# Keeping the delta-rule inverse as 32x32 blocks and transposing it on the vector engine

## The reference

```
L = where(strict, (k_beta @ k.T) * decay, 0)
T = triangular_solve(eye + L, eye, lower=True, unit_diagonal=True)   # the inverse of I + L
u = T @ v_beta ;  w = T @ (k_beta * exp(g_cum))
# then, chunk by chunk: v_new = u - w @ state; o = qd @ state + qk @ v_new; state = ...
```

## Time and profile before

| | before |
|---|---|
| median of 3 runs | 2057.83 us (2057.76 to 2059.85) |
| span of the profiled execution | 2055.0 us |
| the median less that span | 2.8 us |
| heads 0 to 7 of the recurrence | about 549 to 885 us of the span, one each 43.5 us |

### The profile page before, as it was taken

The page is one execution under the profiler, slowest core; times in us unless marked ns, Lnnn a source line. Parts: engine busy times, 40 slices in busy tenths (PEclk is TensorE's granted clock), DMA queues, the critical chain, the costliest instruction groups (busy, mean ns, idle before and its releaser), DMA issues.

```text
span 2055.0 us, 31779 instructions
## 1 busy us (share of the span) xinstructions
PE 2017.8 (98%) x12910; PEld 1621.5 (79%) x12910; DVE 1465.0 (71%) x2281; ACT 569.1 (28%) x994; POOL 354.7 (17%) x320
## 2 busy tenths in 40 slices
PE   8999999999999999999999999999999999999999
PEld 6888788887777777777778877777888888888887
DVE  5766666667877777667888887566656778949973
ACT  2000122222544444324774234444310010000000
POOL 2212111111101110011111211111112122212221
PEclk9999999999999999999999999999999999999999
DMA  4323222222211121122112332111223332322332
GB/s 161 112 92 103 83 90 86 93 83 75 83 60 57 63 68 61 60 72 82 62 63 73 126 98 88 62 48 45 77 82 103 98 103 92 103 92 93 102 97 88
DMA packets 53361, 173.73 MB, mean 85 GB/s; under 512 B 6336, under 2 KB 6720, under 8 KB 53088
## 3 DMA queue, kind: packets, MB, share of 16 engines
q1 hardware_dynamic: 48112, 161.67, 23.9%
q10 hardware_dynamic: 5104, 10.03, 1.8%
HBM read 169.51 MB, written 2.16 MB: 84 GB/s over the span
## 4 chain that ended last, share of the span: by engine, by line
PE 45%; DVE 6%; ACT 2%; issue 1%; DVEq 0%; ACTq 0%
PE ps_lin L1817 13%; PE ps_lin L1818 13%; PE ps_lin L1819 13%; PE ps_att L1863 4%; PE ps_aux L1863 2%; ACT arena L1271 2%; DVE arena L409 1%; DVE w_lo L409 1%; DVE arena L415 1%; DVE arena L897 1%; PE ps_att L1872 0%; DVE y_lo L409 0%; DVE sq L409 0%; DVE xw_lo L415 0%; DVE x L409 0%
## 5 line engine op out<-in xcount | busy, mean ns | idle before, releaser
L1817 PE MATMUL ps_lin<-xw_hi,w_hi 128*128 128x512 f32 (+1 forms) x1728 | 698.5, 404 | 0.0
L1819 PE MATMUL ps_lin<-xw_hi,w_lo 128*128 128x512 f32 (+1 forms) x1728 | 675.0, 391 | 0.0
L1818 PE MATMUL ps_lin<-xw_lo,w_hi 128*128 128x512 f32 (+1 forms) x1728 | 674.0, 390 | 0.0
L391 POOL TENSOR_SCALAR w_hi<-raw 128x1024 fp32r<-128x1024 f32 (+5 forms) x312 | 349.9, 1122 | 1685.1 <-PE ps_lin L1819 1560.5
L409 DVE TENSOR_TENSOR w_lo<-raw,w_hi 128x1024 fp32r<-128x1024 f32 (+2 forms) x344 | 382.3, 1114 | 48.0 <-POOL w_hi L391 17.6
L1271 ACT ACTIVATE arena<-arena 128x512 f32<-128x512 f32 (+7 forms) x331 | 206.4, 631 | 734.3 <-DVE arena L409 357.6
L1819 PEld LDWEIGHTS ps_lin<-xw_hi,w_lo 128*128 128x128 f32 (+1 forms) x1728 | 322.7, 187 | 71.8
L1817 PEld LDWEIGHTS ps_lin<-xw_hi,w_hi 128*128 128x128 f32 (+1 forms) x1728 | 323.1, 187 | 68.4 <-issue 3.7
L1818 PEld LDWEIGHTS ps_lin<-xw_lo,w_hi 128*128 128x128 f32 (+1 forms) x1728 | 323.4, 187 | 61.1
L409 DVE TENSOR_TENSOR arena<-ps_lin,rstd 128x512 f32<-128x512 f32 (+2 forms) x213 | 146.6, 688 | 201.2 <-PE ps_lin L1819 186.7
L1817 PE MATMUL ps_lin<-y_hi,w_hi 128*128 128x512 f32 (+1 forms) x544 | 205.4, 378 | 1.3 <-DVE w_lo L409 1.1
(11 more groups left out here) (175 smaller groups left out, 1697.2 us busy)
## 6 DMA issues: line engine op xcount, KB each, us to landing
raw<-in_w_up SPq DMA_DIRECT2D x44, 512.0 KB, 3.3
raw<-in_conv_w_in SPq DMA_DIRECT2D x32, 512.0 KB, 3.3
raw<-in_fox_w_in SPq DMA_DIRECT2D x32, 512.0 KB, 3.3
raw<-in_gdn_w_in SPq DMA_DIRECT2D x32, 512.0 KB, 3.2
raw<-in_w_gate SPq DMA_DIRECT2D x24, 512.0 KB, 3.2
raw<-in_swa_w_in SPq DMA_DIRECT2D x20, 512.0 KB, 3.2
raw<-in_w_ml SPq DMA_DIRECT2D x16, 512.0 KB, 3.3
raw<-in_w_down SPq DMA_DIRECT2D x16, 512.0 KB, 3.6
```

What stands on the lines that cost most here:

```text
L391: pool.tensor_scalar(w_whole(n, kc * c)[0], w_raw(n, kc * c), 1.0, 0.0, mult, add).then_inc(s("w_rounded"), 1)
L1817: pe.matmul(o, wh, hi, start=first and k == 0, stop=False)
L1818: pe.matmul(o, wh, lo, start=False, stop=False)
L1819: ins = pe.matmul(o, wl, hi, start=False, stop=last and k == kc - 1)
```

## The change

The inverse is kept as 32x32 blocks, in 32 columns a chunk, up to level 4. The products with the identity, their ScalarE copy and the products Y of levels 1 to 4 are gone. VectorE instead copies V into `Uc` itself and turns all 32x32 blocks of `Uc` with one transpose into `Ts`; it does so five times a head, for U0 and for levels 1 to 4. Z and V of levels 1 to 4 have 16 moving columns where they had 32. Level 5 uses 32x32 tiles, and level 6 takes its operands from the new 64x64 blocks `Th` and from `U`, which ScalarE (six diagonal copies and two more) and VectorE (one) put together at level 5. U0 is made by four operations on 32 partitions each where there were two on 64. At level 5 X takes two operations where it took one. The fill between the transpose of U0 and level 1 is gone; level 3 has one more. `LAST_PIECE` is moved to match. At head 0 four memsets stand where there was one.

```diff
-        LEVEL_FILL = (0, 2, 2, 1, 1, 2, 1)
+        LEVEL_FILL = (0, 2, 2, 2, 1, 2, 1)
-        LAST_PIECE.update({LAST_FILL + at: (3 + i // BANKS, i % BANKS) for i, at in enumerate((1, 2, 4, 5, 7, 8))})
+        LAST_PIECE.update({LAST_FILL + at: (3 + i // BANKS, i % BANKS) for i, at in enumerate((1, 3, 4, 6, 7, 9))})
...
 # VectorE, gdn_head
-                for top in (0, HD):
-                    step(tt(U0[top:top + HD], chunks(F["LT"])[top:top + HD, :, top:top + HD], over_chunks(mat("pairs0_ident")[top:top + HD, 0:HD], HD), mult))
-                tt(U0, U0, over_chunks(mat("pairs0_ident")[:, HD:]), add).then_inc(s("gdn_U0"), 1)
+                for at in range(0, P, SQ):
+                    last = tt(U0[at:at + SQ], chunks(F["LT"])[at:at + SQ, :, at:at + SQ], over_chunks(mat("pairs")[at:at + SQ, 0:SQ], SQ), mult)
+                step(last)
+                step(tt(U0, U0, over_chunks(mat("pairs")[:, SQ:2 * SQ]), add))
+                dve.transpose(F["Ts"], F["Uc"]).then_inc(s("gdn_T0"), 1)
...
-                fill(1)
...
+                    elif l == 5:
+                        ts(F["X"][l][SQ:HD, :], ps_att[SQ:HD, 2, 0:NT * SQ], -1.0, mult)
+                        ts(F["X"][l][HD + SQ:, :], ps_att[HD + SQ:, 2, 0:NT * SQ], -1.0, mult).then_inc(s("gdn_X"), 1)
...
-                        dve.wait_ge(s("gdn_TX"), 5 * h + l)
-                        tt(part(F["Tm"]), part(F["Tm"]), ps_att[:, 1, 0:P].rearrange("p (b d) -> p b d", d=d), add).then_inc(s("gdn_T"), 1)
+                        if l < 5:
+                            dve.wait_ge(s("gdn_XU"), 6 * h + l)
+                            step(dve.tensor_copy(part(F["Uc"], 1), new(ps_att[:, 3, :])))
+                            dve.transpose(F["Ts"], F["Uc"]).then_inc(s("gdn_T"), 1)
+                        else:
+                            dve.wait_ge(s("gdn_TX"), h + 1)
+                            dve.tensor_copy(chunks(F["Th"])[SQ:, :, 0:SQ], chunks(ps_att[SQ:HD, 1, 0:NT * SQ])).then_inc(s("gdn_T"), 1)
...
 # ScalarE, gdn_head
-                act.wait_ge(s("gdn_U0T"), h + 1)
-                activation(F["Tm"][:, 0:NT * HD], ps_att[:, 2, 0:NT * HD], ACT.Copy).then_inc(s("gdn_T0"), 1)
...
                     if l == 5:
+                        act.wait_ge(s("gdn_T"), 5 * h + 4)
+                        activation(Th[0:SQ, :, 0:SQ], Ts[0:SQ], ACT.Copy)
+                        activation(Th[SQ:, :, SQ:], Ts[SQ:HD], ACT.Copy).then_inc(s("gdn_Th"), 1)
+                        for at in range(0, P, SQ):
+                            activation(U[at:at + SQ, :, at:at + SQ], Uc[at:at + SQ], ACT.Copy)
...
 # TensorE, gdn_head
-                pe.wait_ge(s("gdn_U0"), h + 1)
-                for c in range(NT):
-                    for top in (0, HD):
-                        rows = slice(top, top + HD)
-                        last = mm(Z[rows, c * HD:(c + 1) * HD], F["Uc"][rows, c * HD:(c + 1) * HD], mat("ident")[rows, rows])
-                last.then_inc(s("gdn_U0T"), 1)
-                fill(1)
...
+                    squares = [(slice(b, b + SQ), slice(c * SQ, (c + 1) * SQ), slice(c * P + b, c * P + b + SQ), c) for c in range(NT) for b in range(0, P, SQ)]
+                    below = [(slice(b, b + SQ), slice(b + SQ, b + 2 * SQ), slice(c * SQ, (c + 1) * SQ), slice(c * P + b + SQ, c * P + b + 2 * SQ)) for c in range(NT) for b in (0, HD)]
...
+                    if l < 5:
+                        for rows, at, of, c in squares:
+                            last = mm(to(V[rows], c), F["X"][l][rows, at], half(F["Uc"][rows, at], 1))
+                    elif l == 5:
+                        for a_, b_, at, of in below:
+                            if b_.start == SQ:
+                                last = mm(Y[b_, at], F["Uc"][b_, at], F["X"][l][b_, at])
+                        last.then_inc(s("gdn_TX"), 1)
+                        for a_, b_, at, of in below:
+                            last = mm(V[a_, at], F["X"][l][b_, at], F["Uc"][b_, at])
```

More of the change, by code:

```diff
@@ L26 @@
 HD = 64
+SQ = 32
 FF = 2816
@@ L2018, in gdn_head @@
                 pe.wait_ge(s("gdn_vb"), h + 1)
-                pe.wait_ge(s("gdn_U0"), h + 1)
-                for c in range(NT):
-                    for top in (0, HD):
-                        rows = slice(top, top + HD)
-                        last = mm(Z[rows, c * HD:(c + 1) * HD], F["Uc"][rows, c * HD:(c + 1) * HD], mat("ident")[rows, rows])
-                last.then_inc(s("gdn_U0T"), 1)
-                fill(1)
                 for l in range(1, 7):
                     d = 1 << l
[L2028 to L2031, removed]
+                    squares = [(slice(b, b + SQ), slice(c * SQ, (c + 1) * SQ), slice(c * P + b, c * P + b + SQ), c) for c in range(NT) for b in range(0, P, SQ)]
+                    below = [(slice(b, b + SQ), slice(b + SQ, b + 2 * SQ), slice(c * SQ, (c + 1) * SQ), slice(c * P + b + SQ, c * P + b + 2 * SQ)) for c in range(NT) for b in (0, HD)]
+                    half = lambda ap, i: ap.rearrange("p (b two d) -> p b two d", two=2, d=d)[:, :, i, :]
+                    to = lambda ap, c: ap[:, c * SQ // 2:(c + 1) * SQ // 2].rearrange("p (b d) -> p b d", d=d)
                     if l == 1:
@@ L2035, in gdn_head @@
                         pe.wait_ge(s("gdn_T"), 5 * h + l - 1)
-                    if l < 6:
-                        for c, rows, b, off in tiles:
-                            last = mm(to(Z[rows], c), F["LT"][rows, c * P + b:c * P + b + n], half(F["Tm"][rows], c * HD, 0))
+                    if l < 5:
+                        for rows, at, of, c in squares:
+                            last = mm(to(Z[rows], c), F["LT"][rows, of], half(F["Ts"][rows, at], 0))
+                    elif l == 5:
+                        for a_, b_, at, of in below:
+                            last = mm(Z[b_, at], F["LT"][a_, of], F["Ts"][a_, at])
+                    else:
+                        pe.wait_ge(s("gdn_Th"), h + 1)
+                        for c in range(NT):
+                            last = mm(Z[HD:, c * HD:(c + 1) * HD], F["LT"][0:HD, c * P + HD:(c + 1) * P], F["Th"][:, c * HD:(c + 1) * HD])
@@ new lines, in gdn_head @@
+                    last.then_inc(s("gdn_XT"), 1)
+                    fill(1)
+                    if l == 5:
+                        pe.wait_ge(s("gdn_QK"), h + 1)
+                    elif l == 6:
+                        pe.wait_ge(s("gdn_U"), 2 * h + 1)
+                    pe.wait_ge(s("gdn_X"), 6 * h + l)
+                    if l < 5:
+                        for rows, at, of, c in squares:
+                            last = mm(to(V[rows], c), F["X"][l][rows, at], half(F["Uc"][rows, at], 1))
+                    elif l == 5:
+                        for a_, b_, at, of in below:
+                            if b_.start == SQ:
+                                last = mm(Y[b_, at], F["Uc"][b_, at], F["X"][l][b_, at])
+                        last.then_inc(s("gdn_TX"), 1)
+                        for a_, b_, at, of in below:
+                            last = mm(V[a_, at], F["X"][l][b_, at], F["Uc"][b_, at])
@@ L2049, in gdn_head @@
[L2049 to L2054, removed]
-                    else:
-                        for c in range(NT):
-                            last = mm(V[0:HD, c * HD:(c + 1) * HD], F["X"][l][HD:, c * HD:(c + 1) * HD], F["Uc"][HD:, c * HD:(c + 1) * HD])
+                            last = mm(V[0:HD, c * HD:(c + 1) * HD], F["X"][l][HD:, c * HD:(c + 1) * HD], F["U"][HD:, c * P + HD:(c + 1) * P])
```

59 lines of the change are left out of this document (25 added, 34 removed).

## The result

| | before | after |
|---|---|---|
| median of 17 runs each | 2056.68 us (2053.94 to 2059.85) | 2060.07 us (2053.17 to 2066.15) |
| ratio, 95% interval | | 1.0018 (1.0011 to 1.0025) |
| span of the profiled execution | 2055.0 us | 2058.3 us |

A forecast was written before the change was run, and what follows sets the result against it. TensorE was taken to set the pace; per middle head 2.80 us saved against 2.96 of waits. Six heads +1.0, head 0 +0.1, last head -1.2: -0.1 on the 2055.0 span, plus 2.8 around it, 2057.7 us; range 2044 to 2068.

The forecast's parts named there:

- The part on VectorE's order: Middle head: 2.80 us of TensorE savings against 2.96 us of new waits for VectorE at levels 1, 4 and 5.
- four operations on 32 partitions: VectorE making U0 ahead of the first X: four operations at 0.32 us each without overlap, 1.28 us.
- first LT to V of level 1: VectorE's stretch in a middle head from the first LT to the start of V of level 1: 5.63 us.
- wait ahead of V of level 1 / 4 / 5: TensorE idle for VectorE at three places of a middle head: 1.56, 0.54 and 0.86 us.
- level 5's saving in Y and V: TensorE at level 5 on 32x32 tiles: Y and V cost 0.91 us, which saves 0.36.
- a head, clock at 1.00: Length of a middle head with TensorE at 2.4 GHz: 43.63 us, a change of +0.17.
- Head 0: First head: no norm product at level 4 (-0.73 us), three more memsets ahead of X (about 0.65): +0.1 us.
- The last head: Last head: VectorE has no pieces, product-to-product latency rules; -1.2 us including 0.36 at level 5.
- my own case: Whole kernel: the forecast of 2057.7 us, with 2053 to 2062 as its own range, chance 0.42.
- The step that failed: Rival "much slower": new waits of 3 us in 43 let the clock fall to 1.2 GHz, over 2068 us, chance 0.06.
- All of it comes through: Rival: the waits fill with work taken to be in the way, about 2036 us, chance 0.12.
- Slower, by the transposes: Rival: a transpose of 4-byte words costs 0.69 us at three tight places a head, about 2066 us, chance 0.22.

The follow-up runs named there:

- experiment 1: Changed kernel with one extra 128x512 float32 product on TensorE in the wait for the first X, heads 0 to 6: 2051.38 us, ratio 0.9975.
- experiment 3: Changed kernel with VectorE's QK moved from in front of the first X to behind level 2's transpose: 2046.57 us, ratio 0.9956.
- experiment 4: Changed kernel with qd and the norm product moved behind level 5's copy on VectorE: 2053.26 us, ratio 0.9984.
- experiment 8: Kernel before the change with VectorE's QK done three times in heads 0 to 6: 2070.10 us, ratio 1.0065.
- experiment 7: Changed kernel with the fills put back where the kernel before had them, the last head's pieces too: 2055.12 us, ratio 0.9996.
- experiment 2: Changed kernel with each of the five block transposes done twice: 2068.29 us, ratio 1.0060.
- experiment 5: Changed kernel with QK behind level 2's transpose, and qd and the norm product behind level 5's copy: 2041.29 us, ratio 0.9925.
- experiment 6: Kernel of experiment 5 with one of VectorE's three pieces ahead of the first X also moved to level 2: 2034.30 us, ratio 0.9894.
- 9: Kernel of experiment 6 with qd at level 2 behind QK, only the norm product behind level 5's copy: 2037.98 us, ratio 0.9911.
- 10: Kernel before the change, VectorE reordered: fourth piece moved to level 1, qd and the norm product to level 5: 2054.80 us, ratio 0.9994.
- 11: Kernel of experiment 9 with qd ahead of QK at level 2 instead of behind it: 2034.50 us, ratio 0.9899.

## Why the prediction was wrong

**The part on VectorE's order held, by its own steps.** Removed products turned into waits behind VectorE's order, at the three places named. The terms, where the timelines above show them:

| term of a middle head | predicted | measured |
|---|---|---|
| four operations on 32 partitions | 1.28 | 1.21, start to start |
| block transpose | 0.31 | 0.31 |
| copy; X | 0.22 to 0.26; 0.22 | 0.23; 0.22 |
| first LT to V of level 1 | 5.63 | 644.70 - 639.28 = 5.42 |
| wait ahead of V of level 1 / 4 / 5 | 1.56 / 0.54 / 0.86 | 1.31 / 0.38 / 0.78 |
| Z of level 1, half the columns | 0.60 | 643.00 - 641.74 - 0.68 = 0.58 |
| Z of level 5 | 0.60 | 659.33 - 658.08 - 0.68 = 0.57 |
| level 5's saving in Y and V | 0.36 | 1.62 - 1.07 = 0.55 |
| V of level 1 to 3; V of level 3 to 5 | 7.34; 7.18 | 7.32; 7.03 (experiment 1: 643.73, 651.05, 658.08) |
| TensorE's busy time | 40.2 | 40.27 |
| a head, clock at 1.00 | 43.63 | 43.06 |

Sixteen columns instead of 32 cost the same, as assumed. The four operations don't overlap: the Trainium skill, "VectorE: DVE Perf Modes", section "Two Vector instructions with no wait between them", has an instruction held when its partitions start in another group of 32, and the trace agrees, 0.30 us from start to start. Two sizes were off: X was followed by V after 0.06 us, not the 0.15 that I took from the row of before, and level 5 saved 0.19 more. From LT to V of level 1 the head is 0.21 shorter than I wrote, from there to level 3 0.02, to level 5 0.15, and behind it 0.19, together the 0.57. Head 0 gained 1.26 where I had +0.1; the clock is low for a part of 540 to 551 us in both profiles, so its start is not cleanly to be compared. The last head gained 1.6 (+2.6 at its start, +1.0 at its end), where I had 1.2. So with the clock as before the changed kernel would have been faster, if by little: its one run at a mean clock of 0.997 took 2053.17 us, 3.5 less than before's median, at the lower edge of what I called my own case (2053 to 2062).

**The step that failed is the clock.** I gave it a chance of 0.06, with "the clock stayed at 1.00 with the waits of before". Those waits were 0.2 us each; I carried their evidence over to one of 1.3, and put the clock into the sum at nothing. I also looked at a middle head alone. In the last head of the same trace the clock is at half for 10 us behind waits of 0.59 and 0.55 us, and my own rows show it: 29 records of 64x64 products at 872.87 take 1.50 us where 32 take 1.12.

The runs show in its place: a wait of 1.3 to 1.6 us in this spot is followed, in part of the heads, by 3.4 us at 1.2 GHz, worth 1.46 us. Experiment 1 fills the wait and the falls go; experiment 3 shortens it to 0.71 and they go from the middle heads; experiment 4 leaves it and they stay; experiment 8 makes it in the kernel before and they come. Counted over the six middle heads of each profile:

| wait ahead of V of level 1 | profiles | heads with a fall behind it |
|---|---|---|
| 1.31 | changed kernel; experiment 4 | 4 of 6; 2 of 6 |
| 1.29 | experiment 7 | 6 of 6 |
| 1.38 | experiment 2 | 3 of 6 |
| 1.57 | experiment 8 | 2 of 6 |
| 0.72 or less | before; experiments 1, 3, 5, 6, 9, 10, 11 | 0 of 48 |

In the profiled execution of the changed kernel the 5.8 us of its four falls are more than the 0.40 of six middle heads, the 1.3 of head 0 and the 1.6 of the last one give together (5.3), so the sign turns within the heads, by 0.5 us. The rest of the +3.3 has other sources (0.5 ahead of head 0, 0.7 and 1.6 behind the heads). The typical run has a lower mean clock than this one (0.992 against 0.993).

**The number was close by luck.** Two errors met: going by the one run at a mean clock of 0.997, the kernel without falls takes about 2053 us, 4.5 under my 2057.7, and the low clock adds about 7 to the typical run.

**The rivals.** "All of it comes through" was wrong for this order of VectorE's work and right for the products: experiment 6 reaches 2034 us. "Slower, by the transposes" named the wrong operation. What decides in which heads the clock falls stays open. In the changed kernel heads 5 and 6 had the same wait of 1.31 without a fall, and head 0 one of 1.38; in head 0 of experiment 3 there was a fall behind 0.78 us, in head 0 of experiment 5 none behind the same wait. The longer waits aren't the ones with more falls either. A part of what experiments 1 and 3 gained by the medians is open as well: the mean clocks of the runs point to falls, but no second profile of the changed kernel shows them.

## What to carry to other kernels

When products leave a saturated engine, look at what its helper does, in order, between the last thing it needs and the first thing it gives; taking foreign work out of that stretch is what collects the saving. Here it made 22 us of gain out of a small loss, with the arithmetic of the changed kernel as it was, and without the removed products the same reordering gave nothing. A new wait like this one of 1.3 us is to be priced with the clock as well as with its length. Before saying that the clock will stay, look over the whole trace for the places where it is low, and at the waits ahead of them, not at one typical stretch alone. Where such a wait can't be avoided, work thrown away in the wait can be cheaper than idleness, as experiment 1 shows.

## What the runs showed of the hardware

- Behind a wait of 1.3 to 1.6 us between small float32 products the clock fell from 2.4 to 1.2 GHz for 3.4 us in 17 of 30 middle heads, 1.46 us each, in kernels with the old and the new products; the same wait passed without a fall in the others (window 821.40 to 825.40 above). None of 48 middle heads with 0.72 us or less there had one. Shorter waits are no safeguard elsewhere: falls stood behind 0.78 us (head 0 of experiment 3), 0.84 us (level 5 in experiment 2) and, for 10 us, behind 0.59 and 0.55 us in the last head of the kernel before.
- Going by the profile, a VectorE product with both inputs in SBUF and GpSimd's rounding exclude each other: whichever starts second lasts longer, by nearly the time for which the two overlap (`qd` 0.65 us longer for 0.79 of overlap, the rounding 0.20 for 0.32). In experiment 6 the norm product took 1.54 beside a rounding of 1.05. The Trainium skill, "SBUF — State Buffer", section "SBUF: two separate sides", calls their shared ports an exclusive lock held for the whole instruction; these rows agree to within 0.15 us.
- A float32 block transpose of 128x128 elements takes 0.31 us, and half the moving columns in a 32x32 float32 product save nothing: sixteen such products cost 0.58 us with 16 columns each, measured from projection to projection, and 0.60 with 32.
